# Order of the condition sums, of the first norm's squares and of the weight loads in a two-block transformer kernel

## The reference, cut to what matters

```python
mod = (c_act @ w_ada[l] + b_ada[l])[:, None, :]
shift1, scale1, gate1, shift2, scale2, gate2 = jnp.split(mod, N_MOD, axis=-1)
h = _rmsnorm(x, g_mix[l]) * (1.0 + scale1) + shift1
proj = h @ w_in[l]
...                                    # gating, stick-breaking, dilated window
x = x + (1.0 + gate1) * y              # y = mixed @ w_out
h = _rmsnorm(x, g_ffn[l]) * (1.0 + scale2) + shift2
up = _causal_dwconv(h @ w_up[l], conv_w[l], conv_b[l])
gate, val = jnp.split(up, 2, axis=-1)
x = x + (1.0 + gate2) * ((jax.nn.silu(gate) * val) @ w_down[l])
```

## Time and profile before

| | us |
|---|---|
| median of 3 runs | 961.06 |
| lowest, highest | 960.05, 962.95 |
| the profiled execution, its own time | 966.07 |
| its span | 964.2 |
| TensorE busy | 926.5 |
| VectorE, ScalarE busy | 616.8, 497.6 |
| bytes moved | 176.91 MB |

### The profile page before, as it was taken

One profiled execution on the slowest core, in us unless ns is written; L12 is line 12 of the kernel. 1 busy time (PEld: TensorE's weight loads), 2 busy tenths in 40 slices (PEclk: granted clock), 3 DMA queues, 4 the chain that ended last, 5 costly groups with the idle time before them and its releaser, 6 DMA issues.

```text
span 964.2 us, 18266 instructions
## 1 busy us (share of the span) xinstructions
PE 926.5 (96%) x7641; PEld 874.7 (91%) x7641; DVE 616.8 (64%) x976; ACT 497.6 (52%) x730; POOL 2.9 (0%) x6
## 2 busy tenths in 40 slices
PE   4799999899999999999999999999999999999997
PEld 2688877799999999877999999999999999999996
DVE  0575664677777677877665666557886765666654
ACT  3446762655555557675644433446556663443341
POOL 1000000000000000000000000000000000000000
PEclk9899999999999999999999999999999999999999
DMA  9997748474555668332375555555452645555531
GB/s 326 325 319 246 248 176 280 166 242 170 179 188 176 217 176 175 88 88 86 114 255 183 176 175 179 194 174 179 130 173 88 219 153 193 178 177 175 181 126 45
DMA packets 132463, 176.91 MB, mean 183 GB/s; under 512 B 19665, under 2 KB 112125, under 8 KB 132253
## 3 DMA queue, kind: packets, MB, share of 16 engines
q1 hardware_dynamic: 131756, 173.97, 55.1%
q10 hardware_dynamic: 624, 1.77, 0.6%
HBM read 174.68 MB, written 1.05 MB: 182 GB/s over the span
## 4 chain that ended last, share of the span: by engine, by line
PE 88%; DVE 5%; ACT 3%; DMA 2%; issue 1%; SPq 0%; DVEq 0%; ACTq 0%
PE psum L1565 26%; PE psum L1557 24%; PE psum L1558 24%; PE psum L1657 2%; DMA raw<-in_w_ada_dram 2%; DVE w_lo L939 1%; PE psum L1561 1%; PE psum L1562 1%; PE psum L1942 1%; PE psum L2063 1%; ACT w_hi L519 1%; PE psum L1997 1%; PE psum L2007 1%; PE psum L2018 1%; ACT arena L804 1%
## 5 line engine op out<-in xcount | busy, mean ns | idle before, releaser
L1557 PE MATMUL psum<-h_hi,w_hi 128*128 128x256 f32 x1352 | 333.4, 285 | 5.1 <-DVE h_lo L1098 4.4
L519 ACT ACTIVATE w_hi<-raw 128x2048 fp32r<-128x2048 f32 (+1 forms) x139 | 264.5, 1904 | 142.9 <-PE psum L1565 114.1
L1558 PE MATMUL psum<-h_lo,w_hi 128*128 128x256 f32 x1352 | 327.3, 280 | 0.0
L939 DVE TENSOR_TENSOR w_lo<-raw,w_hi 128x2048 fp32r<-128x2048 f32 (+1 forms) x139 | 313.3, 2278 | 16.7 <-ACT w_hi L519 16.7
L1557 PEld LDWEIGHTS psum<-h_hi,w_hi 128*128 128x128 f32 x1352 | 256.1, 189 | 16.1 <-issue 12.3
L1558 PEld LDWEIGHTS psum<-h_lo,w_hi 128*128 128x128 f32 x1352 | 256.1, 189 | 0.2
L1565 PE MATMUL psum<-h_hi,w_lo 128*128 128x256 f32 x1352 | 188.2, 280 | 0.3 <-DVE w_lo L939 0.3
L1557 PE MATMUL psum<-a_hi,w_hi 128*128 128x256 f32 x720 | 172.6, 280 | 1.4 <-DVE a_lo L1288 1.2
L1565 PEld LDWEIGHTS psum<-h_hi,w_lo 128*128 128x128 f32 x1352 | 172.0, 189 | 0.6 <-DVE w_lo L939 0.6
L1558 PE MATMUL psum<-a_lo,w_hi 128*128 128x256 f32 x720 | 172.0, 279 | 0.0
L1557 PEld LDWEIGHTS psum<-a_hi,w_hi 128*128 128x128 f32 x720 | 135.4, 188 | 2.0 <-issue 1.9
(11 more groups left out here) (272 smaller groups left out, 778.7 us busy)
## 6 DMA issues: line engine op xcount, KB each, us to landing
raw<-in_mlp_w_in_dram SPq DMA_DIRECT2D x32, 1024.0 KB, 5.6
raw<-in_mlp_w_out_dram SPq DMA_DIRECT2D x32, 1024.0 KB, 7.2
raw<-in_w_ada_dram SPq DMA_DIRECT2D x24, 1024.0 KB, 7.3
raw<-in_w_up_dram SPq DMA_DIRECT2D x22, 1024.0 KB, 5.1
raw<-in_gla_w_in_dram SPq DMA_DIRECT2D x12, 1024.0 KB, 5.4
raw<-in_w_down_dram SPq DMA_DIRECT2D x11, 1024.0 KB, 5.4
raw<-in_w_in_dram SPq DMA_DIRECT2D x10, 1024.0 KB, 8.5
raw<-in_w_out_dram SPq DMA_DIRECT2D x4, 1024.0 KB, 6.4
```

The source lines that it names most:

```text
L519: act.activation(halved(w_hi, m % SPLIT_SLOTS, SPLITS[m]), halved(raw, r % RAW_SLOTS, SPLITS[m]), ACT.Copy).then_inc(*mark("w_hi", m))
L939: dve.tensor_tensor(halved(w_lo, m % SPLIT_SLOTS, key), halved(raw, r % RAW_SLOTS, key), halved(w_hi, m % SPLIT_SLOTS, key).bitcast(F32), ...
L1557: pe.matmul(dst, high, both[0], start=start, stop=False, skip_group_check=True)
L1558: return pe.matmul(dst, high, both[1], start=False, stop=False, skip_group_check=True)
```

## The change

(a) First norm: the squares of `root 0` stand before the copy of the last scale chunk's sum on ScalarE, and TensorE does scale, quarter sums, modulation, total (before: quarter sums, total, modulation). (b) Shift sums 0, 1 stand further ahead; the cast of `in` 0 and its low part have steps of their own (`round`, `round_low`), the low part now behind the second quarter of the input; the high-by-low products of `in` 0 are done in the last two parts. (c) The load of `positions` moves from ScalarE's queue at the start to SyncE's, between loads 9 and 10. (d) `ADA_BESIDE` puts 12 condition chunks, not ten, beside `in` 1 to 9, so two in `in` 2, 5 and 8, none after `in` 10; four remain. Their loads stand: one before val 0, three behind it. Their sums stand around the second norm: two ahead of the quarter sums, one ahead of the total, one behind `scaled`. (e) ScalarE casts no chunk in the step of `in` 9, `out` 0 in that of `in` 10, `out` 1 after the mixers. (f) In the step of `in` 9, stick head 3 comes before the window's softmax.

```diff
@@ weight_stream
-    ada = [("ada", p, q) for p in range(2, 5) for q in range(4)]
+    ada = [("ada", p, q) for p in range(2, 6) for q in range(4)]
...
-        s += [ada.pop(0)] if n > 0 else []
-
-
-    s += [("out", 0), ("out", 1), ("ada", 4, 2), ("out", 2), ("ada", 4, 3), ("ada", 5, 0), ("out", 3),
-          ("ada", 5, 1), ("gate", 0), ("ada", 5, 2), ("val", 0), ("ada", 5, 3)]
+        s += [ada.pop(0) for _ in range(ADA_BESIDE[n])]
+    s += [("out", n) for n in range(4)] + [("gate", 0), ada[0], ("val", 0), *ada[1:]]
@@ module level
+ADA_BESIDE = [0, 1, 2, 1, 1, 2, 1, 1, 2, 1, 0]
@@ schedule
-    s = [("setup",), ("ada", 1, 0), ("ada", 1, 1), ("turn_x",), ("rows", 1), ("ada", 1, 2), ("ada", 1, 3), ("root", 0),
-         ("mod", 1), ("gains", 0), ("shift", 0), ("shift", 1), ("normed", 0), ("mod", 0, 0), ("first", 0), ("shift", 2),
-         ("mod", 0, 1), ("first", 1), ("in_part", 0), ("mod", 0, 2), ("first", 2), ("in_part", 1), ("shift", 3),
-         ("mod", 0, 3), ("first", 3), ("in_part", 2), ("in_part", 3)]
+    s = [("setup",), ("ada", 1, 0), ("ada", 1, 1), ("turn_x",), ("rows", 1), ("ada", 1, 2), ("root", 0), ("ada", 1, 3),
+         ("quarters", 0), ("mod", 1), ("gains", 0), ("total", 0), ("shift", 0), ("normed", 0), ("mod", 0, 0), ("round", 0),
+         ("shift", 1), ("first", 0), ("mod", 0, 1), ("first", 1), ("round_low", 0), ("shift", 2), ("in_part", 0),
+         ("mod", 0, 2), ("first", 2), ("shift", 3), ("in_part", 1), ("mod", 0, 3), ("first", 3), ("in_part", 2), ("in_part", 3)]
...
-             9: [("win_b",), ("stick_a", 4), ("gate_mix",), ("stick_b", 3), ("stick_a", 5)],
+             9: [("stick_a", 4), ("stick_b", 3), ("win_b",), ("gate_mix",), ("stick_a", 5)],
...
-        s += [ada.pop(0)] if n > 0 else []
+        s += [ada.pop(0) for _ in range(ADA_BESIDE[n])]
...
-    s += [("gains", 1), ("ada", 4, 2), ("project", "out", 0), ("ada", 4, 3), ("ada", 5, 0), ("project", "out", 1),
-          ("ada", 5, 1), ("project", "out", 2), ("mod", 4), ("ada", 5, 2), ("project", "out", 3), ("gains", 2)]
-    s += [("root", 1), ("scaled", 1), ("ada", 5, 3)]
+    s += [("gains", 1), ("project", "out", 0), ("project", "out", 1), ("project", "out", 2), ("mod", 4),
+          ("project", "out", 3), ("gains", 2), ("ada", 5, 0), ("ada", 5, 1), ("root", 1), ("quarters", 1), ("ada", 5, 2), ("total", 1),
+          ("scaled", 1), ("ada", 5, 3)]
@@ load_rest (SyncE)
+                sp.dma_start(pos_i[:, :], a["positions"].broadcast_to([P, S])).then_inc(*mark("pos_landed", 0, by=16))
@@ take_in (ScalarE)
-                ahead(("in", n))
+                if n < 9:
+                    ahead(("in", n))
+                elif n == 10:
+                    weights_upto(SPLIT_OF[("out", 0)])
@@ in_part (TensorE)
-                for m in range(2):
-                    for k in (2 * c, 2 * c + 1):
-                        ins = crossed(first_sums[m], wview(w_lo, slot, KT)[:, k, m * P:m * P + P], h_hi[:, k, :],
-                                      k == KT - 1)
...
+                if c == 2:
+                    low_weights(key)
+                    for m in range(2):
+                        low_part(m, range(6))
+                elif c == 3:
+                    for m in range(2):
+                        low_part(m, (6, 7)).then_inc(*mark("job", *key, m))
```

More of the change, by code:

```diff
@@ L591, in setup @@
                 act.dma_start(x_rows, a["x"][0].rearrange("(t p) c -> p t c", p=P)).then_inc(*mark("x_landed", 0, by=16))
-                act.dma_start(pos_i[:, :], a["positions"].broadcast_to([P, S])).then_inc(*mark("pos_landed", 0, by=16))
                 act.wait_ge(*at("cols", 0))
@@ L630, in root, with round_first @@
                     act.activation(work[:, k, :], x_t[:, k, :], ACT.Square).then_inc(*mark("square", i, k))
[L631 to L635, removed]
+            def round_first(n):
+                weights_upto(n)
             def first(c):
@@ L912, in finish @@
                 act.activation(small[:, 72:74], small[:, 70:72], ACT.Exp, scale=-0.5).then_inc(*mark("last_rstd", 0))
-            steps = {"setup": setup, "ada": ada_sums, "turn_x": turn_x, "angles": angles, "root": root, "normed": normed, "shift": shift, "first": first, "scaled": scaled,
+            steps = {"setup": setup, "ada": ada_sums, "turn_x": turn_x, "angles": angles, "root": root, "round": round_first, "shift": shift, "first": first, "scaled": scaled,
                      "split": split, "silu": silu, "unscaled": unscaled,
@@ L1093, in all_normed, with round_low @@
                     normed(i, k)
-                weights_lo_upto(0)
+            def round_low(n):
+                weights_lo_upto(n)
             def low_of_scaled(i, k):
@@ L1519, in _ @@
             steps = {"setup": setup, "rows": columns, "angles": angles, "w_sp": mask_w_sp, "in": take_in, "down": down, "qkv": qkv,
-                     "gla": gla, "mlp_up": mlp_up, "mod": modulation, "gains": gains, "normed": all_normed, "first": first, "scaled": scaled, "rope": rope,
+                     "gla": gla, "mlp_up": mlp_up, "mod": modulation, "gains": gains, "normed": all_normed, "round_low": round_low, "first": first, "scaled": scaled, "rope": rope,
                      "v_norm": v_norm, "gate_mix": gate_mix, "stick_a": stick_a, "stick_b": stick_b,
@@ L1691, in modulation @@
                 ins.then_inc(*mark("job", "mod", p))
-            def root(i):
-                quarters(i)
-                total(i)
             def in_part(c):
@@ L1700, in in_part, with low_part @@
                 slot = weights(key)
+                def low_part(m, tiles):
+                    for k in tiles:
+                        ins = crossed(first_sums[m], wview(w_lo, slot, KT)[:, k, m * P:m * P + P], h_hi[:, k, :], k == KT - 1)
+                    return ins
                 if c == 0:
-                    low_weights(key)
                     first_sums.extend(take(pe, *key, m)[:, 0:S] for m in range(2))
@@ L2085, in _ @@
                      "mod": modulation,
-                     "root": root, "in": take_in, "rope": rope,
+                     "in": take_in, "rope": rope,
                      "gate_mix": gate_mix, "stick_a": stick_a, "stick_b": stick_b, "stick_c": stick_c,
```

3 lines of the change are left out of this document (removed).

## The result

The changed kernel takes 966.18 us, the median of 11 runs (963.46 to 968.49); the kernel before, run beside it, 961.35 (11 runs, 960.05 to 965.28). The prediction had 963.0 and a range of 957.8 to 967.0. The time lies in it, but the likeliest case was "within 0.3%" (0.46 against 0.41 for slower), and the sum of +1.9 us is less than half of what came.

A forecast was written before the change was run, and what follows sets the result against it. TensorE, busy 926.5 of 964.2 us, and its few waits bound the kernel, with one DMA-bound stretch; 0.5 + 0.3 + 1.65 + 1.0 (sums moved ahead of `in` 10) - 7.75 + 2.0 + 4.2 = +1.9, so 963.0 us, range 957.8 to 967.

The forecast's parts named there:

- Part 1: First norm to `in` 3: `in` 2 begins 1.0 us earlier, `in` 3 lands late behind two chunks; loss 0.5 us.
- Part 2: `in` 4 to `in` 10: ScalarE stands for the load of `in` 9, stick steps slip; loss 0.3 us.
- Part 3: `in` 10 to `out` 0: without the sum there TensorE waits for ScalarE's chain and a bank; loss 1.65 us.
- Part 4: Output stage: four sums and the 1.85 us DMA wait with its slow wake go; 7.75 us less.
- Part 5: Second norm: two sums ahead of the quarter sums delay the norm and the first gate product; cost 2.0 us.
- Part 6: Gate 1 and val 1: gate 1's load must wait for val 0's low part, so TensorE waits; cost 4.2 us.
- A: Rival: stages ahead of the output keep their cover, gate 1 costs its first wait alone; 958.2 us, chance 0.17.
- B: Rival: ScalarE bounds the input stage, standing for `in` 7, 9 and 10; 965.3 us, chance 0.2.
- C: Rival: clock falls behind new waits (`in` 3, chunk 53, gate 1) cost up to 1.65 us each; 965.3 us, chance 0.1.
- D: Rival: the first norm's 1.9 us gain stays down the whole kernel; 960.6 us, chance 0.08.

The follow-up runs named there:

- positions_first: Changed kernel with the load of `positions` back at the very start, on ScalarE's queue; 967.98 us, ratio 1.0053 to the kernel before.
- late_only: Changed kernel with the first norm, the parts of `in` 0 and `positions` as in the kernel before; 964.75 us, ratio 1.0028 to the kernel before.
- low_part_early: Changed kernel with the low part of `in` 0 moved right behind the first shift modulation; 962.61 us, ratio 1.0003 to the kernel before.
- double_one_later: Changed kernel with the doubled condition chunk beside `in` 3 instead of `in` 2; 967.37 us, ratio 1.0059 to the kernel before.
- gate1_ahead: Changed kernel with condition chunk 51 loaded ahead of val 0, so gate 1's load waits for sum 51; 963.37 us, ratio 1.0011 to the kernel before.
- late_and_gate1: Kernel before with all edits after the first norm, plus condition chunk 51 loaded ahead of val 0; 963.03 us, ratio 0.9999 to the kernel before.
- first_norm_only: Kernel before with only the edits around the first norm (schedule, `in_part`, place of `positions`); 963.53 us, ratio 1.0017.

## Why the prediction was right or wrong

**What bounds the kernel.** Right in the main: a few waits carry most of the effect, and the stretch up to 60 us is bound by DMA.

**Part 1, the step that failed.** I read the low part of `in` 0 as ending "near 34.2 as before", and it did (the load of `in` 1 went out at 34.35, before at 34.06). From that I concluded that `in` 2 "lands where it did, 50.1, or up to 1.2 later". It landed 3.1 later, TensorE waited 3.70 us, and the clock fell. The forecast gave a gain of 1.0 for the start of `in` 2; it began 1.2 later than before (55.15 against 53.96). The 3.1 us are 0.3 for the later load of `in` 1, about 1.2 (by one trace) for `positions`, which halves the flow while it moves (219 GB/s at 38 to 40, before 463), and some 1.6 that the sum had nowhere: the load of `in` 2 took 16.1 us in the three traces read with these edits, 15.3 in positions_first, 13.7 before and 13.8 in late_only, and what in the order of the first norm makes it longer stays open.
Also missed was a cure. The condition chunks had landed by 32, and the DMA engines stood from then to 36 instead of from 33 (0.00 at 32 to 34, 0.23 at 34 to 36). That longer gap did not delay `in` 2 against before, since the load of `in` 1 ends it at the same time in both; but low_part_early, which closes it, lets the loads go out 4.7 us sooner and takes 4.0 us off. And on TensorE's side, coming 4 us earlier through `in` 0 and 1 was no reserve: it only met a landing that had not come earlier, and made a gap in front of `in` 2 with a half-clock stretch behind it.
By the medians part 1 is half of the miss. The first norm's edits cost 1.6 (0.4 to 2.9) where its terms gave 0 to 0.5, and the late edits 2.7 (1.5 to 3.8) where parts 2 to 6 gave 1.4. That the time fell in the range (957.8 to 967.0) owes something to its width.
The doubled chunk, to which I gave 3.0 us of landing and the wait of 1.2 at `in` 3, did that to the landing (62.29; I had 61.2) and nothing to the time: double_one_later.

**Part 2.** Forecast +0.3, measured -0.4. ScalarE stood 2.15 us for `in` 9, not 5: the cast began at 113.50, where I had 111.5, but ScalarE came to it only at 111.35, 7.7 us later than before, behind a TensorE that was over 4 us late by then instead of 3.4. The stick wait came to 0.30 instead of 0.67; the sign was wrong, the size small.

**Part 3.** +1.65 forecast, +1.6 measured; the waits in front of the window's products were 0.63 and 0.33 us.

**Part 4.** -7.75 and -8.0. No DMA wait stands between 140 and 172.

**Part 5, undersized.** Forecast +2.0 with chunk 53 landing at T+6.4, "summed before the first product". The sums, quarters and total went in the order written, a little sooner (the total begins at 176.04 and takes 0.70, so it is done at T+4.3; I had T+4.8). Chunk 53 landed at T+8.0: its load left behind sum 50 near 173.6 and took 6.9 us, where I had some 5. It became the last thing that TensorE waited for, 3.79 us, and sum 53 behind it took 1.94 us at clock 0.50 instead of 1.06. The Trainium skill, "DMA: Bandwidth & Descriptors", section "Anatomy of one DMA", would have 4.4 us as an estimate for 1 MB, written for another issuing engine; the trace does not agree, since from 140 to 215 no such load of the changed kernel came in under 5.0.

**Part 6, right in mechanism, oversized by 1.1.** Gate 1's load left at val 0's low part, TensorE stood 1.27 us for the bank (forecast 2.6) and 0.91 for the low part (1.2), and val 0's last low products to gate 1's first took 5.39 us instead of 2.80; val 1 added 0.4. The forecast of the bank's wait was too long since TensorE itself came 0.8 later out of part 5, and val 0's low part only 1.4 later behind T than before (184.62 - 172.47 = 12.15, before 10.76), where I had 2.0. gate1_ahead and late_and_gate1 measure the wait apart: 3.3 and 2.8 us.

**The rivals.** A did not come. B: ScalarE did stand, for `in` 9 and 10, without harm. C, the clock, is what came on top of the forecast, and its 965.3 (B had the same by another way) was nearest to the measured time, in part by luck, since the rest of the sum was off too: the clock fell behind the wait for `in` 2 and behind that for chunk 53, and not behind gate 1's 1.27. The Trainium skill, "TensorE: Matmul & The Clock Gate", section "HAM oscillation", warns of such gaps between bursts, and here the trace agrees at both. C had `in` 3, not `in` 2, for its first place. D: the first norm's gain was not only lost in the full DMA queue, it turned into a loss (first_norm_only, +1.6, 0.4 to 2.9).

The chance of 0.41 for slower was fair. What the sum lacked is visible in its form: part 4 counted the half-clock stretch behind the old 1.85 us wait as gained, while every new wait was priced at its length alone. In the changed kernel's trace the clock fell behind two new waits. The slow stretches stood in a rival with a chance of 0.1; they belonged in the sum.

## What to carry to other kernels

Where a stretch is bound by DMA, do not ask when a load's data are wanted, but what frees the slot it goes into: here the step that frees it was moved by 4.7 us on an idle VectorE (32.04 to 27.35) and brought 4 to 5 us, the largest gain of one edit in these runs. When loads wait for slots, two neighbours in the load order may hang on steps 13 us apart; look up for each load which step frees its slot, and put the one wanted first behind the one freed first. Work done earlier in front of a wait that stays only makes the gap longer; price a gap with the slow matmuls behind it.

## What the runs showed of the hardware

The price of a fall of the clock. Behind the 3.70 us wait for `in` 2 and the 3.79 us wait for chunk 53 the granted clock was 0.50 (55 to 60) and 0.66 (180 to 185, mean); behind the two waits of gate 1 (1.27 and 0.91) it stayed at 1.00. Added up over 25 to 240 us (1 - PEclk in steps of 5 us), the clock stood at half for a loss of 5.1 us in the kernel before: 3.4 in the first norm and 1.7 behind the 1.85 us wait of the earlier trace rows. In the changed kernel it is 8.5: 3.4 in the first norm, 3.4 around the start of `in` 2 (0.6 of that while TensorE was mostly idle), 1.7 behind the wait for chunk 53. That this difference, 3.4, is as large as that of the two traces at 213 us does not make it the cause: gate1_ahead has 10.2 and stands 0.4 us ahead of before there (209.24). double_one_later has 10.2 too, with a fall behind gate 1's waits, 2.19 and 0.44 us there. Other falls come and go with the execution: before, low_part_early and double_one_later had one near 450 us, behind the same 2.2 us wait behind which the changed kernel's profiled execution had none. At 1.7 us each they may be a good part of the 5 us by which runs of one kernel differ.

Matmuls at the same granted clock of 1.00 took about 1% longer in one execution than in another (172 against 174 in 20 us; 1.6 us over some 160 us). So a span says less than a checkpoint, and a checkpoint late in the program less than an early one; but the early one moves too, by the 2.15 us at 71 to 73 between two executions of the same program.

A 1 MB load took 16.1 us from issue to landing for `in` 2 of the changed kernel, with two others and a strip of small packets around it, 13.7 for the same load before, and 4.8 to 5.4 with no other 1 MB load beside it.
